# First attention stage: logits, transposes and values in turned order every second step, values one step later, dilated logits of two heads alternating

## The chip, the cores and the metric

One core of a Trainium2 chip. The metric is the device time of one execution in microseconds (us). Three executions of the kernel before were timed.

## What is computed

A model of two blocks, each of two layers, on 512 tokens of width 1024. Each layer of the first block begins with a mixer of three kinds of attention on the same normed input; the change lies in the stage that computes these, and nowhere else. The second block (stick-breaking, latent and recurrent mixers) is not touched.

```python
BLOCK = 128
def hybrid_mixer(u, pos, w_in, idx_k_norm, sinks, w_a, w_b, w_c, w_o):
    (aq, ak, av, iq, ik, iw, bq, bk, bv, cq, ck, cv, gates) = split_columns(u @ w_in)
    ...
    o_a = dsa_attention(qa, ka, av, iqr, ikr, iw * IDX_HEADS ** -0.5)   # 6 heads, keys picked by top-k
    o_b = dilated_attention(...)             # 3 groups of 4 heads: window 128 step 1, 512 step 4, 2048 step 16
    o_c = sink_window_attention(...)         # 8 heads, window 128, a sink in the denominator
    g = jax.nn.sigmoid(gates.reshape(Bsz, L, N_BRANCHES, D_MODEL))
    merged = (g[:, :, 0] * (o_a.reshape(Bsz, L, -1) @ w_a) + g[:, :, 1] * (o_b.reshape(Bsz, L, -1) @ w_b)
              + g[:, :, 2] * (o_c.reshape(Bsz, L, -1) @ w_c))
    return merged @ w_o
```

In each of the three, a block of 128 queries takes logits against its keys, a masked softmax over them, and the product of the weights with the values. The dilated one joins its three groups with weights from their log-sums; since all three are then exponentials over one common denominator, the kernel treats the keys of the three groups as one row.

## The kernel before, in words

The kernel is written engine by engine: each engine has its own queue of instructions, which it works through in order, and they meet at semaphores. The layer loop is unrolled, so the stage stands twice in the program and in the trace, with the same lines.

**Units.** The work of the stage is a list of 36 units (`units`). A unit is two heads and 128 queries: 8 dilated ones ("B", 768 logits per query: 512 of group 1, and 128 each of groups 2 and 3), 16 sliding-window ones ("C", 128 or 256 logits) and 12 top-k ones ("A", 128 to 512 logits). They are dealt in the pattern B C C A, B C C A A, so the dilated units are 0, 4, 9, 13, 18, 22, 27 and 31. The first units of each kind are short (128), the later ones longer: C is 256 wide from unit 10 on, A is 256 wide at 12, 16, 17, 384 wide at 21, 25, 26 and 512 wide at 30, 34, 35.

**Steps.** `steps()` yields for each step the unit that each stage of a software pipeline works on: s0 (this step's unit, logits), s1 (one unit back, exponentials), s2 (three back, transposes), s3 (four back, values), s4 (five back, the output's copy). All queues run over the same steps:

- TensorE: `logits(s0)`, `turn(s2)`, `values(s3)`. Logits contract over the 64 dimensions of a head, so the two heads lie on the two halves of the partitions (`half(e)`); a dilated unit makes two 512-wide products (part 0, L986) and then, head by head, two 128-wide ones for groups 2 and 3 (part 1, L991). `turn` transposes the softmax weights in blocks of 128 x 128 (L1010). `values` multiplies them with the values; the two heads write the two halves of the output's partitions (L1031).
- VectorE: for s0 a masked, scaled copy of the logits out of PSUM with a row minimum (L1119), then the minimum that ScalarE waits for (`row_min`, L1127 or L1131 to L1133; a top-k unit has only the count); for s4 the low part of the output, `o_lo` (L1143), after ScalarE's high part (`o_kept`); for s2 the copy of a dilated unit's transposes to `pt` (L1148); for s1 the reciprocal of the denominator (L1155) and, for a dilated unit, the scaling of one of its heads (L1160).
- ScalarE: for s1 the exponentials of both heads (L1066, in a window unit after the sink's at L1064), once `row_min` is there; for s4 the high part of the output, `o_hi` (L1072); for s2 the copies of the transposes of units that aren't dilated (L1079).
- GpSimd: the scaling of the other heads (L1090), after the reciprocal.
- SP: once the logits of unit 31 are done, the fetch of the next block's first weights.

**Buffers.** The eight PSUM banks are dealt round by `Banks.plan` in the order in which TensorE fills them; `bank_to_fill` waits until the bank's last content was read, `bank_filled` until it is full. The logits after the mask (`sc`) have four buffers, `pt` has two: the copy for unit k waits for the values of unit k-2.

These are the lines of VectorE's step before, in their order (bodies cut):

```python
for s0, s1, s2, s3, s4 in steps():
    if s0 is not None:   # L1119 masked copy and row minimum, then row_min
    if s4 is not None:
        dve.wait_ge(S["o_kept"], k + 1)
        nc.vector.tensor_tensor(o_lo[:, tile, cols], ...)
    if s2 is not None and pt_by_dve(s2):   # L1148 copies
    if s1 is not None:   # L1155 reciprocal, L1160 scaling
```

Of the kernel before, what the change touches and what calls it, by code (L numbers as in the profile page):

```python
# [10 lines left out]
ALU = mybir.AluOpType  # L11
# [4 lines left out]
P = 128  # L16
L = 512
D = 1024
DC = D // P
TB = L // P  # L20
# [106 lines left out]
def build(nc, d, debug=False, stop=None):  # L127
    ctx = ExitStack()
    with ctx:
# [469 lines left out]
        for layer in range(DEPTH):  # L599
# [301 lines left out]
            def steps():  # L901

                for k in range(len(units) + 5):
                    yield [k - lag if 0 <= k - lag < len(units) else None for lag in (0, 1, 3, 4, 5)]
# [13 lines left out]
            def turned(k):  # L918


                n = 2 * unit_width(units[k]) // P
                return [range(at, min(at + 4, n)) for at in range(0, n, 4)]

            jobs = Banks()
            for s0, s1, s2, s3, s4 in steps():
                if s0 is not None:
                    for part in range(2 if units[s0][0] == "B" else 1):
                        for e in range(2):
                            jobs.plan(("logits", s0, part, e))
                if s2 is not None:  # L930
                    for part in range(len(turned(s2))):
                        jobs.plan(("pt", s2, part))
                if s3 is not None:
                    jobs.plan(("o", s3))
# [23 lines left out]
            with nc.Block() as block:  # L958
# [10 lines left out]
                def _(pe, jobs=jobs):  # L969

                    def logits(k):
                        br, j, b = units[k]
                        w = unit_width(units[k])
                        for part in range(2 if br == "B" else 1):
                            for e in range(2):
# [9 lines left out]
                                elif part == 0:  # L985
# [49 lines left out]
                    for s0, s1, s2, s3, s4 in steps():  # L1035
                        if s0 is not None:
                            logits(s0)
                        if s2 is not None:
                            turn(s2)
                        if s3 is not None:  # L1040
                            values(s3)
# [52 lines left out]
                def _(dve, jobs=jobs):  # L1094
# [3 lines left out]
                    for s0, s1, s2, s3, s4 in steps():  # L1098
                        if s0 is not None:
                            k = s0  # L1100
                            br, j, b = units[k]
                            x, w = exps(k)
                            if k >= 4:

                                turn_done(dve, jobs, k - 4)
                            mn = per_unit(MIN_AT, k)
                            part0, part1 = (small[:, PART_AT + 4 * (k % 2) + 2 * i:PART_AT + 4 * (k % 2) + 2 * i + 2] for i in range(2))
                            if br == "B":
                                mask = [cst[:, C1_DIL + b * L:C1_DIL + (b + 1) * L], cst[:, C1_DIL16:C1_DIL16 + 256]]
                            elif br == "C":  # L1110
                                mask = [cst[:, C1_WIN + 256 - w:C1_WIN + 256]]
                            else:
                                mask = [causal if b == 0 else score[:, b - 1, 0:w]]
                            for part, m in enumerate(mask):
                                n = m.shape[1]
                                for e in range(2):
                                    bank = bank_filled(dve, jobs, ("logits", k, part, e))
                                    out = (mn if br == "A" else part1 if part else part0)[:, e:e + 1]
                                    i = nc.vector.tensor_tensor_reduce(out=x[:, e, part * L:part * L + n], in0=ps[:, bank, 0:n], in1=m,  # L1119
                                                                       scale=-(HD ** -0.5), scalar=-NEG, op0=ALU.add, op1=ALU.min,  # L1120
                                                                       accum_out=out)
                                    i.then_inc(read[bank], 1)
                            for part in range(len(mask)):
                                for e in range(2):
                                    dve.wait_ge(*read_of(jobs, ("logits", k, part, e)))
                            if br == "B":
# [2131 lines left out]
```

## Time and profile before

| what | us |
|---|---|
| median of 3 executions | 3410.07 |
| lowest and highest | 3406.38, 3415.58 |
| the profiled execution's own time | 3413.77 |
| its span, first to last instruction | 3411.7 |
| TensorE busy in the span | 3296.1 (97%) |
| VectorE, ScalarE, GpSimd busy | 1709.9, 1338.0, 974.0 |
| attention stage, first layer | from 228.5 to 338.4 |
| attention stage, second layer | from 1123.9 to 1235.6 |

The profile is of one execution. Busy time of TensorE is modelled: products are pipelined, and the end of one is drawn after the start of the next, so in the timeline the time from start to start is what counts. One fp32 product of logits or values leaves two records. The granted clock is the share of TensorE's full clock that the chip let it have. "Idle before" is the engine's idle time just ahead of an instruction, with what ended it; "issue" means that the profile shows nothing that was waited for.

### The profile page before, as it was taken

How to read it: one execution, taken by the hardware profiler on the slowest of the kernel's cores; microseconds unless marked ns; L12 is line 12 of the kernel's file. 1: busy time of each engine (PE TensorE's matmuls, PEld its weight loads, DVE VectorE, ACT ScalarE, POOL GpSimd, SP SyncE). 2: the span in 40 equal slices, each digit the busy share in tenths (PEclk: the TensorE clock that was granted, in tenths of full speed). 3: DMA queues.
4: the chain of work that ended last, by engine and by line, in shares of the span. 5: the costliest groups of instructions: out<-in, count | busy, mean ns of one | idle time of the engine just before them, and what ended most of it. 6: DMA issues, size and time to landing. Idle time of an engine off the chain costs nothing. (4 is left out here: it accounts for less than half of the span.)

```text
span 3411.7 us, 54710 instructions
## 1 busy us (share of the span) xinstructions
PE 3296.1 (97%) x22568; PEld 2713.9 (80%) x22568; DVE 1709.9 (50%) x2688; ACT 1338.0 (39%) x2039; POOL 974.0 (29%) x613
## 2 busy tenths in 40 slices
PE   8989999999999899999999999899999999899998
PEld 7776887888778678878887869888887768888887
DVE  5887334313259753451413675554444566454454
ACT  5647333323255553332324362343324453343322
POOL 2336002444443430034443341241101342141100
PEclk9999999999999899999999999899999999999999
DMA  4200332223221023222233100212222200112222
GB/s 158 75 25 28 105 105 88 99 88 108 88 99 62 1 80 105 104 87 99 87 125 102 62 1 4 100 50 94 91 99 95 95 1 4 76 47 103 90 95 74
DMA packets 63905, 264.36 MB, mean 77 GB/s; under 512 B 17472, under 2 KB 32192, under 8 KB 35008
## 3 DMA queue, kind: packets, MB, share of 16 engines
q1 hardware_dynamic: 63680, 261.12, 22.0%
q8 instruction: 170, 2.79, 0.4%
q14 instruction: 55, 0.45, 0.0%
HBM read 259.01 MB, written 2.10 MB: 77 GB/s over the span
## 5 line engine op out<-in xcount | busy, mean ns | idle before, releaser
L1487 POOL TENSOR_TENSOR w_lo_f<-raw_f,w_hi_f 128x2048 fp32r<-128x2048 f32 x60 | 275.7, 4596 | 379.7 <-ACT w_hi_f L389 379.7
L401 PE MATMUL ps<-u_hi,w_hi_d 128*128 128x512 f32 (+1 forms) x768 | 291.3, 379 | 7.0 <-POOL u_lo L2950 5.6
L402 PE MATMUL ps<-u_lo,w_hi_d 128*128 128x512 f32 (+1 forms) x768 | 287.3, 374 | 0.0
L403 PE MATMUL ps<-u_hi,w_lo_d 128*128 128x512 f32 (+1 forms) x768 | 287.2, 374 | 0.0
L389 ACT ACTIVATE w_hi_f<-raw_f 128x2048 fp32r<-128x2048 f32 x64 | 121.9, 1908 | 253.6 <-PE ps L403 243.8
L401 PE MATMUL ps<-hid_hi,w_hi_f 128*128 128x512 f32 x512 | 199.2, 389 | 0.0
L402 PE MATMUL ps<-hid_lo,w_hi_f 128*128 128x512 f32 x512 | 199.2, 389 | 0.0
L403 PE MATMUL ps<-hid_hi,w_lo_f 128*128 128x512 f32 x512 | 199.2, 389 | 0.0
L1514 DVE TENSOR_TENSOR hid<-hid 128x512 f32<-128x512 f32 x64 | 119.1, 1860 | 137.3 <-ACT hid L1463 135.5
L655 POOL TENSOR_TENSOR w_lo_a<-raw_a,w_hi_a 128x2048 fp32r<-128x2048 f32 x28 | 129.0, 4609 | 200.1 <-ACT w_hi_a L651 200.1
L401 PEld LDWEIGHTS ps<-u_hi,w_hi_d 128*128 128x128 f32 x768 | 146.5, 191 | 35.3 <-POOL u_lo L2950 7.4
L401 PE MATMUL ps<-u_hi,w_hi_f 128*128 128x512 f32 x448 | 174.3, 389 | 0.0
L403 PE MATMUL ps<-u_hi,w_lo_f 128*128 128x512 f32 x448 | 174.3, 389 | 0.0
L402 PE MATMUL ps<-u_lo,w_hi_f 128*128 128x512 f32 x448 | 174.3, 389 | 0.0
L1090 POOL TENSOR_SCALAR sc<-sc,small 128x256 f32<-128x256 f32 (+4 forms) x120 | 133.2, 1124 | 128.3 <-DVE small L1155 128.2
L402 PEld LDWEIGHTS ps<-u_lo,w_hi_d 128*128 128x128 f32 x768 | 147.0, 191 | 25.5 <-issue 0.5
L2962 POOL TENSOR_TENSOR hid_lo<-ge,hid_hi 128x512 f32 (+1 forms) x44 | 57.1, 1299 | 385.4 <-ACT hid_hi L2906 385.4
L403 PEld LDWEIGHTS ps<-u_hi,w_lo_d 128*128 128x128 f32 x768 | 146.9, 191 | 25.0
L395 DVE TENSOR_TENSOR w_lo_d<-raw_d,w_hi_d 128x2048 fp32r<-128x2048 f32 x44 | 106.3, 2416 | 103.9 <-ACT w_hi_d L389 103.3
L401 PE MATMUL ps<-u_hi,w_split_c 128*128 128x512 f32 x384 | 149.6, 390 | 2.1 <-SPq L228 1.0
L402 PE MATMUL ps<-u_lo,w_split_c 128*128 128x512 f32 x384 | 149.4, 389 | 0.0
L403 PE MATMUL ps<-u_hi,w_split_c 128*128 128x512 f32 x384 | 149.4, 389 | 0.0
(466 smaller groups left out, 8583.1 us busy)
## 6 DMA issues: line engine op xcount, KB each, us to landing
raw_d<-in_w SPq DMA_DIRECT2D x70, 1024.0 KB, 4.8
raw_f<-in_w SPq DMA_DIRECT2D x64, 1024.0 KB, 4.8
raw_c<-in_w SPq DMA_DIRECT2D x40, 1088.0 KB, 5.0
raw_a<-in_w SPq DMA_DIRECT2D x22, 1024.0 KB, 4.9
raw_p<-in_w SPq DMA_DIRECT2D x22, 1024.0 KB, 4.8
raw_a<-in_w SPq DMA_DIRECT2D x18, 512.0 KB, 4.8
wo_raw<-in_w SPq DMA_DIRECT2D x4, 1024.0 KB, 5.9
h<-in_x SPq DMA_DIRECT2D x8, 256.0 KB, 4.5
```

Source lines behind the costliest of these rows:

```text
L389: nc.scalar.activation(hi[:, k % 2, 0:width], raw[:, k % raw.shape[1], 0:width], ACT.Copy).then_inc(S["w_hi"], 1)
L395: nc.vector.tensor_tensor(lo[:, k % 2, 0:width], raw[:, k % raw.shape[1], 0:width], hi[:, k % 2, 0:width].bitcast(F32), ALU.subtract).then ...
L401: nc.tensor.matmul(out, w_hi, x_hi, start=start, stop=False)
L402: nc.tensor.matmul(out, w_hi, x_lo, start=False, stop=False)
L403: return nc.tensor.matmul(out, w_lo, x_hi, start=False, stop=stop)
L655: eng.tensor_tensor(WA_lo[:, i % 4, :], WA_raw[:, i % 4, :], WA_hi[:, i % 3, :].bitcast(F32), ALU.subtract)\
L1090: nc.gpsimd.tensor_scalar(x[:, e, 0:w], x[:, e, 0:w], per_unit(INV_AT, k)[:, e:e + 1], None, ALU.mult)\
L1487: nc.gpsimd.tensor_tensor(WF[2][:, k % 2, :], WF[0][:, k % 2, :], WF[1][:, k % 2, :].bitcast(F32), ALU.subtract).then_inc(S["w_lo"], 1)
L1514: nc.vector.tensor_tensor(x, x, x, ALU.mult).then_inc(S["relu_kept"], 1)
L2962: nc.gpsimd.tensor_tensor(at(hid2_lo, k), ge, at(hid2_hi, k).bitcast(F32), ALU.subtract)\
```

## The change

Three edits in this stage, and nothing outside it. TensorE's order is logits, transposes, values in even steps and values, transposes, logits in odd ones (`products()`, which the plan of the banks follows too). The lags of values and of the output's copy go from 4 and 5 to 5 and 6, so there is one step more. The four small products of a dilated unit alternate between its heads. VectorE's step is put in another order: `o_lo` comes first, then in odd steps the copy of a dilated unit's transposes, then the reduction of the logits, then in even steps that copy, and last, as before, the reciprocal. The bodies of the reduction and of the copy become functions (`reduce`, `turned_out`), unchanged. The queues of ScalarE, GpSimd and SP are not edited; they take the new lags from `steps()`.

```diff
-                for k in range(len(units) + 5):
-                    yield [k - lag if 0 <= k - lag < len(units) else None for lag in (0, 1, 3, 4, 5)]
+                for k in range(len(units) + 6):
+                    yield [k - lag if 0 <= k - lag < len(units) else None for lag in (0, 1, 3, 5, 6)]
...
-            for s0, s1, s2, s3, s4 in steps():
-                if s0 is not None:
-                    for part in range(2 if units[s0][0] == "B" else 1):
+
+            def products():
+
+                for n, (s0, s1, s2, s3, s4) in enumerate(steps()):
+                    kinds = (("logits", s0), ("turn", s2), ("values", s3))
+                    yield from (x for x in (kinds if n % 2 == 0 else kinds[::-1]) if x[1] is not None)
+
+            for what, k in products():
+                if what == "logits":
+                    for part in range(2 if units[k][0] == "B" else 1):
                         for e in range(2):
-                            jobs.plan(("logits", s0, part, e))
...
+                            if part == 1:
+                                banks = [bank_to_fill(pe, jobs, ("logits", k, part, e)) for e in range(2)]
+                                rows = slice(b, L, TB)
+                                for g in (1, 2):
+                                    for e, bank in enumerate(banks):
+                                        m = nc.tensor.matmul(ps[:, bank, (g - 1) * P:g * P], qk[half(e), T_BQ + 2 * g + j, rows],
+                                                             qk[half(e), T_BK + 2 * g + j, rows], start=(g == 1), stop=(g == 2),
+                                                             skip_group_check=True)
+                                        if g == 2:
+                                            m.then_inc(full[bank], 1)
+                                continue
...
-                                else:
-                                    for g in (1, 2):
-                                        rows = slice(b, L, TB)
-                                        m = nc.tensor.matmul(ps[:, bank, (g - 1) * P:g * P], qk[r, T_BQ + 2 * g + j, rows],
-                                                             qk[r, T_BK + 2 * g + j, rows], start=(g == 1), stop=(g == 2),
-                                                             skip_group_check=True)
-                                    m.then_inc(full[bank], 1)
...
-                    for s0, s1, s2, s3, s4 in steps():
-                        if s0 is not None:
-                            logits(s0)
-                        if s2 is not None:
-                            turn(s2)
-                        if s3 is not None:
-                            values(s3)
+                    for what, k in products():
+                        if what == "logits":
+                            logits(k)
+                        if what == "turn":
+                            turn(k)
+                        if what == "values":
+                            values(k)
...
-                    for s0, s1, s2, s3, s4 in steps():
-                        if s0 is not None:
-                            k = s0
...
+                    def turned_out(s2):
+
+                        if s2 is not None and pt_by_dve(s2):
+                            for part in range(len(turned(s2))):
+                                bank, dst, src = pt_copy(dve, jobs, s2, part)
+                                nc.vector.tensor_copy(dst, src).then_inc(read[bank], 1)
+
+                    for n, (s0, s1, s2, s3, s4) in enumerate(steps()):
                         if s4 is not None:
                             k = s4
                             bank = bank_filled(dve, jobs, ("o", k))
...
                             dve.wait_ge(S["o_kept"], k + 1)
                             nc.vector.tensor_tensor(o_lo[:, tile, cols], ps[:, bank, 0:P], o_hi[:, tile, cols].bitcast(F32),
                                                     ALU.subtract).then_inc(read[bank], 1)
-                        if s2 is not None and pt_by_dve(s2):
-                            for part in range(len(turned(s2))):
-                                bank, dst, src = pt_copy(dve, jobs, s2, part)
-                                nc.vector.tensor_copy(dst, src).then_inc(read[bank], 1)
+                        if n % 2 == 1:
+                            turned_out(s2)
+                        if s0 is not None:
+                            reduce(s0)
+                        if n % 2 == 0:
+                            turned_out(s2)
                         if s1 is not None:
                             k = s1
                             den = per_unit(DEN_AT, k)
```

## Rows read from the trace of the kernel before

**Rows 1.** Busy time by stretch: us; per engine busy (instructions); clock, DMA, GB/s.

```profile
core 0: us, PE busy (x) PEld busy (x) DVE busy (x) ACT busy (x) POOL busy (x), PEclk, DMA share, GB/s
228.50:254.20 25.70, 19.84 (x151) 15.03 (x153) 16.69 (x80) 13.79 (x50) 12.27 (x14) 0.80 0.00 1
254.20:329.60 75.40, 74.55 (x604) 51.30 (x601) 60.02 (x247) 52.50 (x167) 52.50 (x44) 0.95 0.08 31
329.60:338.40 8.80, 7.41 (x94) 5.98 (x92) 6.02 (x18) 6.13 (x16) 1.82 (x2) 1.00 0.01 3
244.00:252.00 8.00, 6.09 (x58) 4.13 (x58) 6.43 (x32) 5.72 (x26) 4.97 (x6) 1.00 0.00 1
256.00:264.00 8.00, 7.68 (x32) 4.32 (x33) 5.65 (x29) 5.98 (x22) 5.63 (x5) 0.59 0.01 3
1123.90:1153.20 29.30, 23.38 (x151) 17.12 (x153) 16.92 (x80) 13.66 (x50) 12.30 (x14) 0.71 0.00 1
1153.20:1226.80 73.60, 71.72 (x604) 49.57 (x601) 59.69 (x246) 52.21 (x167) 52.48 (x44) 1.00 0.08 32
```

**Rows 2.** Timeline of TensorE, first layer: start, length in us, line, records.

```profile
269.42 0.70 PE L982 MATMUL ps<-qk 64*128 64x256 f32 x4
270.06 0.66 PE L1010 MATMUL ps<-cst,sc 128*128 128x128 f32 x4
271.23 0.70 PE L982 MATMUL ps<-qk 64*128 64x256 f32 x4
...
305.14 1.30 PE L991 MATMUL ps<-qk 64*128 64x128 f32 x8
306.38 0.66 PE L1010 MATMUL ps<-cst,sc 128*128 128x128 f32 x4
```

**Rows 3.** Waits of the values' weight loads, 228.5 to 338.4 us: total us, times, longest.

```profile
PEld ps L1031 <- issue: 6.3, 34, 0.4
```

**Rows 4.** Timeline of VectorE, first layer: start and length in us.

```profile
280.41 0.69 DVE L1119 CUSTOM_DVE_ANT_0 sc<-ps,cst 128x512 f32<-128x512 f32 x1 [1.55 <-PE ps L986]
...
284.95 0.29 DVE L1143 TENSOR_TENSOR o_lo<-ps,o_hi 128x128 fp32r<-128x128 f32 x1 [0.17 <-ACT o_hi L1072]
285.16 0.15 DVE L1155 RECIPROCAL small<-small 128x2 f32<-128x2 f32 x1
...
289.21 1.88 DVE L1148 COPY pt<-ps 128x512 f32<-128x512 f32 x3
...
297.11 0.42 DVE L1119 CUSTOM_DVE_ANT_0 sc<-ps,cst 128x256 f32<-128x256 f32 x1
...
298.97 0.56 DVE L1119 CUSTOM_DVE_ANT_0 sc<-ps,score 128x384 f32<-128x384 f32 x1
...
325.78 0.69 DVE L1119 CUSTOM_DVE_ANT_0 sc<-ps,score 128x512 f32<-128x512 f32 x1 [0.47 <-PE ps L979]
```

**Rows 5.** Timeline of ScalarE, first layer.

```profile
282.74 0.94 ACT L1066 ACTIVATE sc<-sc,small 128x768 f32<-128x768 f32 x1
...
284.59 0.25 ACT L1072 ACTIVATE o_hi<-ps 128x128 fp32r<-128x128 f32 x1
...
298.38 0.20 ACT L1064 ACTIVATE small<-small 128x2 f32<-128x2 f32 x1
...
299.47 0.25 ACT L1072 ACTIVATE o_hi<-ps 128x128 fp32r<-128x128 f32 x1
...
300.09 0.61 ACT L1066 ACTIVATE sc<-sc,small 128x384 f32<-128x384 f32 x1 [0.37 <-DVEq L1136]
...
301.31 0.25 ACT L1072 ACTIVATE o_hi<-ps 128x128 fp32r<-128x128 f32 x1
...
327.17 0.72 ACT L1066 ACTIVATE sc<-sc,small 128x512 f32<-128x512 f32 x1 [0.95 <-DVEq L1136]
...
328.60 0.25 ACT L1072 ACTIVATE o_hi<-ps 128x128 fp32r<-128x128 f32 x1
```

**Rows 6.** Timeline of GpSimd, first layer: both heads of a 256-wide unit.

```profile
291.45 1.83 POOL L1090 TENSOR_SCALAR sc<-sc,small 128x256 f32<-128x256 f32 x2 [1.62 <-DVE small L1155]
```

More of the change, by code:

```diff
@@ L924, in build @@
             jobs = Banks()
[L925 to L934 removed]
+            def products():
[5 more added lines that the diff above has]
+                    for part in range(2 if units[k][0] == "B" else 1):
+                        for e in range(2):
+                            jobs.plan(("logits", k, part, e))
+                if what == "turn":
+                    for part in range(len(turned(k))):
+                        jobs.plan(("pt", k, part))
+                if what == "values":
+                    jobs.plan(("o", k))
             def o_place(unit):
@@ L1097, in _ @@
                                                                 prm[:, P1_SINK:P1_SINK + C_HEADS], -1.0, None, ALU.mult)))
-                    for s0, s1, s2, s3, s4 in steps():
-                        if s0 is not None:
-                            k = s0
[L1101 to L1126, printed above, removed]
-                                nc.vector.tensor_tensor(mn, part0, part1, ALU.min).then_inc(S["row_min"], 1)
-                            elif br == "C":
-                                sink = slice(2 * j, 2 * j + 2)
-                                dve.wait_ge(*own.up(nc.vector.tensor_tensor(mn, part0, prm[:, P1_NSINK:P1_NSINK + C_HEADS][:, sink],
-                                                                            ALU.min)))
-                                nc.vector.tensor_tensor(per_unit(SINK_AT, k), mn, prm[:, P1_SINK:P1_SINK + C_HEADS][:, sink],
-                                                        ALU.add).then_inc(S["row_min"], 1)
-                            else:
-                                dve.sem_inc(S["row_min"], 1)
@@ new lines, in reduce @@
+                    def reduce(k):
+                        br, j, b = units[k]
+                        x, w = exps(k)
+                        if k >= 4:
+                            turn_done(dve, jobs, k - 4)
+                        mn = per_unit(MIN_AT, k)
+                        part0, part1 = (small[:, PART_AT + 4 * (k % 2) + 2 * i:PART_AT + 4 * (k % 2) + 2 * i + 2] for i in range(2))
+                        if br == "B":
+                            mask = [cst[:, C1_DIL + b * L:C1_DIL + (b + 1) * L], cst[:, C1_DIL16:C1_DIL16 + 256]]
+                        elif br == "C":
+                            mask = [cst[:, C1_WIN + 256 - w:C1_WIN + 256]]
+                        else:
+                            mask = [causal if b == 0 else score[:, b - 1, 0:w]]
+                        for part, m in enumerate(mask):
+                            n = m.shape[1]
+                            for e in range(2):
+                                bank = bank_filled(dve, jobs, ("logits", k, part, e))
+                                out = (mn if br == "A" else part1 if part else part0)[:, e:e + 1]
+                                i = nc.vector.tensor_tensor_reduce(out=x[:, e, part * L:part * L + n], in0=ps[:, bank, 0:n], in1=m,
+                                                                   scale=-(HD ** -0.5), scalar=-NEG, op0=ALU.add, op1=ALU.min,
+                                                                   accum_out=out)
+                                i.then_inc(read[bank], 1)
+                        for part in range(len(mask)):
+                            for e in range(2):
+                                dve.wait_ge(*read_of(jobs, ("logits", k, part, e)))
+                        if br == "B":
+                            nc.vector.tensor_tensor(mn, part0, part1, ALU.min).then_inc(S["row_min"], 1)
+                        elif br == "C":
+                            sink = slice(2 * j, 2 * j + 2)
+                            dve.wait_ge(*own.up(nc.vector.tensor_tensor(mn, part0, prm[:, P1_NSINK:P1_NSINK + C_HEADS][:, sink],
+                                                                        ALU.min)))
+                            nc.vector.tensor_tensor(per_unit(SINK_AT, k), mn, prm[:, P1_SINK:P1_SINK + C_HEADS][:, sink],
+                                                    ALU.add).then_inc(S["row_min"], 1)
+                        else:
+                            dve.sem_inc(S["row_min"], 1)
```

7 lines of the change are left out of this document (3 added, 4 removed).

## Prediction

> **What bounds the kernel now.** I read the busy time of each engine by stretches first, for this stage alone. The attention stage runs once per layer of the first block, twice in all. Its steady stretch, from the start of VectorE's first logits reduction of unit 9 to that of unit 35, lasts 75.4 us in the first layer and 73.6 us in the second; before it lie 25.7 us of start-up, behind it 8.8 us of tail [rows 1]. The reader is to see that TensorE is busy for 74.55 of 75.40 us there, while VectorE has 60.02, ScalarE 52.50 and GpSimd 52.50: TensorE sets the pace and each other engine has room, if its work may overlap. Then the timeline of TensorE: a step of a 256-wide unit (logits, transposes, values) goes from 269.42 to 271.23, which is 1.81 us [rows 2]. Then the waits of the weight loads: before values, whose kind of product differs from what ran before, they sit for nothing the profile shows, 0.19 us at a time (6.3/34) [rows 3]. I take that as the price of going from one kind of product to another.
>
> **What the change takes out of TensorE.** Turning every second step round puts values beside values and logits beside logits: two changes of kind per step in place of three, some 36 x 0.19 = 6.8 us per layer. The two heads' dilated logits alternate: four 128-column products take 1.24 us (305.14 to 306.38), two of 256 columns on the two halves 0.64 us (269.42 to 270.06) [rows 2]. The same columns can't cost less than the latter, so each of 8 dilated units saves between 0 and 0.60 us, at most 4.8 us per layer. The Trainium skill (TensorE: Matmul & The Clock Gate, What overlaps and what doesn't) says that a weight load overlaps running products only if its row group differs. By that rule the sum for TensorE would stand at the 4.8 us end, and these rows agree. I cost both savings at nothing in the total, because the next part takes TensorE off the path.
>
> **What the change adds: a wait at the head of VectorE's step.** Values move from lag 4 to lag 5, the write of o_lo from 5 to 6, and on VectorE o_lo moves ahead of the reduction of this step's logits. ScalarE's queue is not reordered: in step n it does the exponentials of unit n-1, then o_hi of unit n-6, then its copies of transposes. VectorE's step n now begins with o_lo of unit n-6, which waits for that o_hi. It stands behind the exponentials of n-1, and these need the row minimum of n-1 from VectorE's step before. So from step 6 on each reduction starts only when the exponentials of the unit before are done: reduce(n-1), exp(n-1), o_hi, o_lo, reduce(n), one after another on two engines. Before, reduce(n) ran beside exp(n-1), and only o_lo, behind it, waited. Queued behind the wait are now the dilated copy (odd steps), the reduction, the reciprocal and the scaling; ScalarE waits for them, GpSimd for the reciprocal, TensorE for GpSimd and for banks.
>
> One link of this chain, from reduction to reduction, for each kind of unit:
> - Sliding-window unit, 256 wide: reduction at 297.11, ScalarE starts at 298.38 (1.27); o_hi starts at 299.47 and takes 0.25 (1.34) [rows 4, 5]. From the end of an o_hi (284.59 + 0.25) to its o_lo at 284.95 is 0.11, and what follows an o_lo starts 0.21 later (285.16) [rows 4, 5]. Together 2.93.
> - Dilated: 280.41 to 282.74 (2.33), to the end of o_hi at 284.84 (2.10), plus 0.32: 4.75.
> - Top-k unit, 384 wide: 298.97 to 300.09 (1.12), to 301.56 (1.47), plus 0.32: 2.91. 512 wide: 325.78 to 327.17 (1.39), to 328.85 (1.68), plus 0.32: 3.39. For 256 I take as much less again, 2.43 [rows 4, 5].
>
> Units 9 to 34 lead from reduce(9) to reduce(35): 6 dilated, 12 window, 3 + 3 + 2 top-k units: 28.5 + 35.2 + 7.3 + 8.7 + 6.8 = 86.5 us. The copies of dilated units (three in 1.88 us [rows 4]) come on top. In odd steps they now stand between o_lo and the reduction, for units 18 and 22: 2 x 1.88 = 3.8. In even steps they run while ScalarE works and stick out: 1.88 plus some 0.4 for the reciprocal and its neighbours, against ScalarE's part of the link, leaves about 0.85 with a 256-wide and 0.4 with a 512-wide unit, two of each: 2.5. Sum 92.8 us, which is 17.4 over the first layer's 75.4 and 19.2 over the second's 73.6.
>
> Start-up: logits of step 3 now stand behind the transposes of unit 0, and the copies of units 0 and 4 before reduce(3) and reduce(7). This can cost nothing or both copies, 3.8 us; I take 1.8 in the first layer. In the second, whose start-up is already 3.6 us longer (29.3 against 25.7 us [rows 1]), I take 0, with the same two ends. Tail: one step more, with little in it. It lies between nothing and a values block with its copies, 2 us; I take 1 each. SP's fetch of the next weights waits for the logits of unit 31 and moves with them, four links ahead of its first reader: nothing. If that cover went, the next block would wait for it. GpSimd keeps its 52.5 us of work inside 92.8: nothing.
>
> Total: 17.4 + 1.8 + 1 + 19.2 + 0 + 1 = 40.4 us. Against the profiled execution's own 3413.77 us (span 3411.7 and 2.1 around it) this is 3454.2. That execution lies 3.7 us above the median of the three runs, so against the median the forecast is 3410.07 + 40.4 = **3450 us**, 1.2% slower. A measurement of this kernel can tell about 0.3%, 10.2 us, from no change.
>
> **Rivals.** *TensorE stays the bound, faster.* If ScalarE reached o_hi before VectorE needs it, the step would be TensorE's, and both savings would count: 6.8 and up to 4.8 us per layer, 23 us in all, 3387 us. The place is the gap at each change of kind [rows 3]; the point is where a link becomes shorter than TensorE's step. Against it: 2.93 us against 1.81. The Trainium skill (TensorEngine Tiling (Array Packing), Key Properties) says that a change of tiling mode drains TensorE. By that rule alone the change would win, at the 3387 us just given; the 0.19 us gaps agree with it. Chance 0.04.
>
> *GpSimd's scaling becomes the wait, the chain through o_lo does not bind.* Transposes of an even unit now come a step earlier after the odd unit's logits. From those logits it takes 1.27 and some 0.2 us on VectorE, then two heads in 1.83 us on GpSimd [rows 6], 3.3 us; TensorE has a logits, a transposes and two values blocks to do, 0.64 + 0.58 + 1.0 = 2.2 us [rows 2]. 1.1 us are missing in the 7 of 13 pairs of steps without long work to cover it, 8 us per layer; about 7 come back as fewer changes of kind (13 x 2 x 0.19 = 4.9) and as alternation. The time would be about 3412 us, the same by measure. For it: the loop is there. Against it: the other one is longer, 5.86 us for two window steps against 3.3 + 0.58 + 0.64 = 4.5. Chance 0.05.
>
> *The clock falls too.* Between 244 and 252 us TensorE was busy for 6.09 of 8 us at the full clock; from 256 to 264 it was granted 0.59 on average, between its levels of 1.2 and 2.4 GHz [rows 1]. With the chain it would be busy for 71.7 of 92.8 us, a share like that before the fall. At the lower level TensorE's work doubles, so it becomes the bound again if over 0.29 of its 71.7 us falls there (92.8/71.7 - 1). With half of it there, the stretch is 107.6 us, 14.8 more per layer: 3480 us. For it is the start-up of either layer, granted 0.80 in the first; against it, the clock came back, since the whole stretch has 0.95 and the second layer's 1.00. Chance 0.08.
>
> **How the numbers follow.** The chain has 0.83. Its own range: 3434 with no odd or even copies in the chain, no start-up cost and no tail; 3456 with both copies in both start-ups. The range given, 3432 to 3472, adds part of the clock's case and leaves out the two quicker rivals. Faster by over 0.3% has 0.04, within 0.3% 0.05, slower 0.91.
>
> **What would show it.** In the changed profile o_lo should have a long idle time before it, ended by ScalarE's o_hi, in nearly every step from 6 on, some 1 us with a window unit; ScalarE's exponentials should wait for VectorE's row minimum. From reduce(9) to reduce(35) should be about 93 us, with one window step near 2.9 us, and TensorE should show idle time before logits and transposes. The four dilated products should take between 0.64 and 1.24 us. The prediction is wrong if o_lo waits little, if the stretch stays near 75 us, or if TensorE is busy throughout at a low clock.

## The result, and the profile after

The changed kernel takes 3501.82 us (median of 4 runs, 3493.79 to 3505.21) beside 3410.26 us of the kernel before on the same chip: ratio 1.0267, 95% interval 1.0252 to 1.0282. It is slower by 91.6 us; the forecast was slower by 40.4 us. The direction was right, the size was not, and 3502 lies outside the range of 3432 to 3472.

The busy time by stretch of the changed kernel, with the columns of [rows 1]; in order, start-up, steady stretch and tail of the first layer, then start-up and steady stretch of the second:

```profile
228.20:260.80 32.60, 22.68 (x154) 16.67 (x156) 16.94 (x80) 13.83 (x50) 12.32 (x14) 0.69 0.00 1
...
260.80:374.70 113.90, 79.27 (x602) 59.31 (x598) 59.65 (x247) 52.81 (x167) 53.29 (x45) 0.84 0.06 21
...
374.70:384.70 10.00, 7.03 (x93) 6.07 (x93) 6.08 (x17) 5.54 (x15) 1.48 (x2) 1.00 0.01 2
...
1170.60:1203.00 32.40, 23.47 (x154) 17.23 (x156) 17.02 (x80) 13.87 (x50) 12.32 (x14) 0.63 0.00 1
...
1203.00:1317.50 114.50, 78.88 (x602) 59.33 (x598) 59.61 (x246) 52.94 (x167) 53.21 (x45) 0.85 0.05 21
```

Against [rows 1] the steady stretch grew by 38.5 us (113.90 - 75.40) and 40.9 us (114.50 - 73.60), the start-up by 6.9 us (32.60 - 25.70) and 3.1 us (32.40 - 29.30), and the tail of the first layer by 1.2 us. These account for nearly all of the 91.6 us: the loss is in this stage. VectorE, ScalarE and GpSimd have the work they had, to within 1 us; TensorE is busy for 79.27 of 113.90 us in place of 74.55 of 75.40, at a granted clock of 0.84. So no engine is full: the stage waits.

The waits of the changed kernel from 228 to 390 us (total us, times, longest):

```profile
DVE o_lo L1162 <- ACT o_hi L1083: 51.6, 30, 4.3
PE ps L1021 <- DVE o_lo L1162: 30.1, 11, 4.0
ACT pt L1090 <- PE ps L1042: 27.5, 11, 4.5
PEld ps L1021 <- POOL sc L1101: 24.3, 11, 4.4
ACT sc L1077 <- DVEq L1146: 22.5, 10, 4.3
ACT sc L1077 <- DVE small L1137: 16.1, 6, 3.8
ACT small L1075 <- DVE small L1143: 11.1, 10, 1.6
PE ps L1042 <- DVE o_lo L1162: 7.5, 4, 2.4
```

The first row is the forecast chain: VectorE's o_lo at the head of its step waits for ScalarE's o_hi in 30 of 36 steps, and the exponentials (L1075, L1077) wait for VectorE's minima. Three more kinds of wait have no price in the forecast: TensorE's transposes (L1021) and its values (L1042) wait for o_lo, and ScalarE's copies (L1090) wait for TensorE's values. Two steps of the timeline, 280.66 to 286.77 and 286.77 to 289.79, show how they hang together (start, length in us, engine and line; in brackets the idle time before it and what ended it):

```profile
280.66 0.29 DVE L1162 TENSOR_TENSOR o_lo<-ps,o_hi 128x128 fp32r<-128x128 f32 x1 [2.17 <-ACT o_hi L1083]
281.10 1.08 PE L1021 MATMUL ps<-cst,sc 128*128 128x128 f32 x4 [4.01 <-DVE o_lo L1162]
282.11 2.50 PE L1042 MATMUL ps<-pt,bv 128*64 128x128 f32 x24
...
284.72 0.60 ACT L1090 ACTIVATE pt<-ps 128x512 f32<-128x512 f32 x1 [4.16 <-PE ps L1042]
285.22 0.19 ACT L1075 ACTIVATE small<-small 128x2 f32<-128x2 f32 x1
...
286.29 0.38 ACT L1083 ACTIVATE o_hi<-ps 128x128 fp32r<-128x128 f32 x1
...
286.77 0.39 DVE L1162 TENSOR_TENSOR o_lo<-ps,o_hi 128x128 fp32r<-128x128 f32 x1 [3.95 <-ACT o_hi L1083]
...
289.43 0.25 ACT L1083 ACTIVATE o_hi<-ps 128x128 fp32r<-128x128 f32 x1
289.79 0.29 DVE L1162 TENSOR_TENSOR o_lo<-ps,o_hi 128x128 fp32r<-128x128 f32 x1 [1.21 <-ACT o_hi L1083]
```

From 286.77 to 289.79 is a window step that is the chain and nothing else: 3.02 us, where 2.93 were forecast. From 280.66 to 286.77 is one of 6.11 us. Step 14 begins it: o_lo of unit 8 ends and frees its PSUM bank. The transposes of unit 11 were dealt that very bank, so TensorE stood idle for 4.01 us until then. The transposes run at the lower clock of 1.2 GHz (granted 0.50 from 281.10 to 282.11): 1.08 us, where four take 0.66 at the full clock in [rows 2]. The values of unit 9 run mostly at it (granted 0.59 from 282.11 to 284.60): 2.50 us, where the kernel before takes 1.53 us for such values at the full clock:

```profile
267.96 1.53 PE L1031 MATMUL ps<-pt,bv 128*64 128x128 f32 x24
```

ScalarE's copy of unit 11 goes into the operand buffer that the values of unit 9 still read, one of two, so it starts after them, at 284.72. The exponentials of unit 14 stand behind this copy, o_hi of unit 9 behind the exponentials, and the next o_lo behind that. So a second loop goes o_lo, bank, transposes and values, copy, exponentials, o_hi, o_lo; where it closes here, the step is twice as long. The wait of this copy for the values is not needed for the loop: experiment 7 takes it away and gains little.

The order in which the kernel deals its banks fixes how often such a meeting comes. In the changed kernel 13 products per layer are dealt a bank whose last content is an output with its o_lo in the same step; 11 of them are transposes, as many as the waits of L1021 for o_lo. With the old order and the same lags there is none.

### The profile page after: what moved, and what is told of

Its sections match the earlier page's. It is cut to its first block and busy times, and to the rows that moved or that the text cites. A ratio compares the mean times of both kernels' runs of the same rounds, so it can differ in the third digit from the quotient of the medians.

```text
span 3503.4 us, 54724 instructions
## 1 busy us (share of the span) xinstructions
PE 3310.3 (94%) x22568; PEld 2735.3 (78%) x22568; DVE 1709.0 (49%) x2688; ACT 1338.0 (38%) x2039; POOL 974.9 (28%) x613
```

## The experiments

None of these kernels leaves out anything that the reference computes. They undo or do one part each. "Before" is the run of the kernel before on the same chip.

**1. The split first, alone.** On the kernel before, only VectorE's o_lo moves ahead of the reduction; lags, order and banks stay.

```diff
 for s0, s1, s2, s3, s4 in steps():
+    if s4 is not None:
+        dve.wait_ge(S["o_kept"], k + 1)
+        nc.vector.tensor_tensor(o_lo[...], ...)
     if s0 is not None:
```

> The kernel before with one edit: VectorE writes o_lo ahead of the reduction of the step's logits. Order of TensorE, lags, banks as before. Theory: the chain is there without the turned order; links of 86.5 us from unit 9 to 34 and about 5 us of dilated copies that stick out, against 75.4 and 73.6 us now: 3435 to 3455 us. Rival (the turned order is what costs): 3405 to 3415 us, as before.

Measured: 3452.75 us, before 3410.78, ratio 1.0125 [1.0108, 1.0142]: 42 us slower. Busy time of its steady stretch in the first layer, columns as in [rows 1]:

```profile
258.30:349.70 91.40, 76.52 (x607) 51.74 (x608) 58.66 (x247) 52.67 (x167) 53.05 (x45) 0.94 0.07 26
```

The longest wait of its stage, VectorE's o_lo for ScalarE (total us, times, longest, as in all fences of waits):

```profile
DVE o_lo L1105 <- ACT o_hi L1072: 36.5, 27, 2.4
```

What follows: the chain exists, and the sum of its links was right: 91.4 us (92.6 in the second layer), where this run's own expectation of 86.5 and about 5 us makes 91.5. But it is worth 42 us, not 92.

**2. Values one step later, alone.** On the kernel before, lags 5 and 6 in place of 4 and 5. Then the same with two short operand buffers more, for units of up to 256 columns, so that nearly every copy waits for values of four units before.

```diff
-    yield [... for lag in (0, 1, 3, 4, 5)]
+    yield [... for lag in (0, 1, 3, 5, 6)]
```
```diff
+pt_short = [place("pt_2", 38584, 512), place("pt_3", 34488, 512)]
-b, m, _ = jobs.at["o", k - 2]
+b, m, _ = jobs.at["o", PT_BEFORE[k]]
```

> The kernel before with nothing changed but the values (and with them the split of their output) one step later, lags 5 and 6 in place of 4 and 5; order of the kinds, VectorE's places and the alternation as before. Theory (ScalarE's copy into the values' operand buffer, of which there are two, now waits for values of its own step, and the next exponentials stand behind it): slower, about where the run with the order of before and the new lags was (3443), that is 3435 to 3450, with ScalarE's copies ended by TensorE's values in 20 us or more of the stage of layer 1, where the kernel before shows little of this. Rival (a later step only gives slack; what cost there was VectorE's split behind the reduction with two banks): 3405 to 3415.

> The kernel before with the values one step later, as in the run with that alone, and two short buffers more for the values' operand, so that a copy waits for values of four units before in nearly all cases. Theory (the loss by the lag alone is the wait of the copies on the two buffers): back to 3405 to 3416, ScalarE's copies no longer ended by values. Rival (the loss by the lag alone is something else, as the output's bank held a step longer): within 5 us of the run with the lag alone.

Measured: the later step alone 3424.49 us, before 3412.2, ratio 1.0038 [1.0024, 1.0051]; with more buffers 3411.48 us, ratio 0.9994 [0.9985, 1.0004]. The waits of ScalarE's copies with the later step alone:

```profile
ACT pt L1079 <- PE ps L1031: 27.5, 18, 3.3
```

With more buffers no such row is left; the copies wait only for their own transposes, as in the kernel before:

```profile
ACT pt L1090 <- PE ps L1021: 19.3, 15, 5.1
```

What follows: the later step costs 12 us, less than the 23 to 38 that the theory's 3435 to 3450 make, and all of it by the two buffers, as the theory had it. The forecast had counted the later values as moving o_lo's lag and had not looked at the buffers.

**3. The turned order.** First alone: on the kernel before, with the alternation, VectorE's copies at their new places and two banks for the values alone, but the old lags and the split behind the reduction. Then the other way round: the changed kernel with the old order in every step, all else as changed.

```diff
-kinds if n % 2 == 0 else kinds[::-1]
+kinds
```

> The kernel before with the turned order of logits, transposes and values in every second step, VectorE's copies at their places of after, the alternation and banks of their own for the values, but with the old lags 4 and 5 and the split behind the reduction: the turned order without the later step. Theory (in a step pair the values of two units then stand next to each other, and the second waits for transposes made right ahead of them to be copied out by ScalarE, over 1 us at each pair, with the split behind a reduction that waits for logits behind the values): slower, 3440 to 3480. Rival (the order alone saves its 0.19 us at each change of kind and costs nothing): 3400 to 3411.

> The changed kernel with logits, transposes, values in this order in every step; split first on VectorE, values one step later, alternation and VectorE's copies as changed, banks shared as in the kernel before. Theory (38 us of the loss come from the turned order: it deals the banks so that transposes meet a bank that is freed only behind the split at the head of the same step): the sum of the two single costs, 3410 + 42 + 12 = 3464, within 12. Rival (split first and later values lengthen each other through the shared banks whatever the order): 3485 or more.

Measured: the order alone 3475.58 us, before 3412.2, ratio 1.018 [1.0163, 1.0197]; the changed kernel with the old order 3458.9 us, before 3411.95, ratio 1.0141 [1.0125, 1.0158]. Waits with the order alone:

```profile
PE ps L1043 <- DVE o_lo L1167: 21.3, 20, 1.9
...
PEld ps L1043 <- ACT pt L1091: 16.2, 10, 2.1
```

Waits of the changed kernel with the old order:

```profile
DVE o_lo L1162 <- ACT o_hi L1083: 40.5, 31, 3.7
...
ACT pt L1090 <- PE ps L1042: 17.5, 11, 3.8
...
PE ps L1021 <- DVE o_lo L1162: 2.8, 4, 1.8
```

Busy time of its steady stretch:

```profile
257.30:352.40 95.10, 79.30 (x628) 52.60 (x626) 58.93 (x248) 52.47 (x167) 53.24 (x46) 0.93 0.07 25
```

What follows: this is the run that divides the loss. In the old order split and later step together cost 47.0 us (3458.9 - 3411.95); turning the order adds 44.6 (91.6 - 47.0), give or take some 8 us by the two intervals. The transposes' waits for o_lo fall from 30.1 to 2.8 us when the order is turned back. Turning the order without the later step is worse still, 63 us slower, but that run has a second cost in it: its o_lo stands behind the reduction, and values wait for it for 21.3 us. The first kernel of experiment 6 differs from it by the later step alone and is 46.7 us slower than before (3456.99 - 3410.26). So the missing step accounts for some 17 of the 63 us; there values stand right behind the transposes' copies and wait for ScalarE (16.2 us).

**4. Cutting the loops in the changed kernel.** ScalarE's o_hi ahead of its exponentials cuts the chain; banks 6 and 7 for the values alone, the other six for the rest, cut the bank loop.

```diff
 for s0, s1, s2, s3, s4 in steps():
+    o_hi(s4)
     exps(s1)
-    o_hi(s4)
```
```diff
-jobs = Banks()
+jobs = Banks(count=6)
-jobs.plan(("o", k))
+jobs.fills[6 + k % 2] += 1
+jobs.at["o", k] = (6 + k % 2, jobs.fills[6 + k % 2], 0)
```

> The changed kernel with one edit: ScalarE writes o_hi before the exponentials of the step, not behind them. Theory (the serial chain reduce, exp, o_hi, o_lo, reduce, which the banks make worse): the chain is cut, o_lo's waits on o_hi fall from 52 us per layer to under 10, and the time falls by at least 80 us, to between 3385 and 3420 us. Rival (the turned order itself costs the time, by GpSimd's scaling that must now fit between logits and the next transposes but one): the time stays over 3470 us, and transposes wait for GpSimd as long as now.

> The changed kernel with one edit: values have two PSUM banks of their own (one for even, one for odd units), everything else goes round in the other six. Theory (the chain costs some 40 us, and what lies above it is TensorE waiting for banks that the late o_lo holds, which holds up transposes, ScalarE's copies and so the exponentials): TensorE's waits on o_lo, 40 us per layer, nearly vanish, and the time falls to 3440 to 3465 us. Rival A (the banks only show the chain's lateness): 3490 to 3510 us. Rival B (without the banks there is no chain either): under 3420 us.

> The changed kernel with both cuts: ScalarE writes o_hi before the exponentials, and values have two PSUM banks of their own. Theory (two costs, the chain through o_hi and the banks that o_lo holds, and nothing else): from reduce(9) to reduce(35) 70 to 76 us, TensorE's waits on o_lo under 3 us per layer, 3395 to 3415 us in all. Rival (the turned order itself is slower, GpSimd's scaling between logits and transposes): the stretch stays over 79 us, 3420 us or more, with transposes waiting for GpSimd over 8 us per layer.

Measured: o_hi first 3438.57 us, ratio 1.0079 [1.0062, 1.0096]; own banks 3465.95 us, ratio 1.0158 [1.0141, 1.0175] (before 3410.78 for both); both 3427.93 us, before 3410.26, ratio 1.0054 [1.0038, 1.0071]. The waits in the first layer's stage with o_hi first:

```profile
DVE o_lo L1162 <- ACT o_hi L1074: 13.4, 12, 2.4
...
PE ps L1021 <- DVE o_lo L1162: 10.9, 9, 1.6
```

The same waits with own banks:

```profile
DVE o_lo L1163 <- ACT o_hi L1084: 39.4, 31, 2.3
...
PE ps L1043 <- DVE o_lo L1163: 17.6, 13, 3.2
```

Busy time of the steady stretch with own banks:

```profile
259.40:354.70 95.30, 73.81 (x602) 52.78 (x600) 59.01 (x247) 51.70 (x166) 52.98 (x45) 0.93 0.07 25
```

The longest waits with both cuts:

```profile
PEld ps L1022 <- POOL sc L1102: 12.5, 17, 2.8
PE ps L1022 <- POOL sc L1102: 9.5, 10, 2.0
DVE o_lo L1163 <- ACT o_hi L1075: 5.9, 6, 1.7
...
PE ps L1043 <- DVE o_lo L1163: 4.3, 6, 1.2
```

What follows: with own banks the stretch falls from 113.9 to 95.3 us, that of the changed kernel in the old order with shared banks (95.1): the chain is left, the second loop is gone (36 us in all). The values still wait for o_lo for 17.6 us, against the expectation, so a wait for o_lo does not cost its length by itself. Cutting the chain is worth more, 63 us; read from the queues, the bank loop passes through the same exponentials and is loosened with it. The expectation was 80 us at least, and o_lo still waits for o_hi for 13.4 us where under 10 were expected. Both cuts together give 74 us, not 99: the two loops share links. They miss the expected 3395 to 3415 us as well. The rival's sign, transposes waiting for GpSimd for over 8 us, is there, and experiment 8 tries it.

**5. Controls.** On the kernel before, only the banks for values; and only the alternation of the dilated logits.

> The kernel before with one edit: values have two PSUM banks of their own, the rest goes round in six. A control: what the banks alone do. Theory (in the order of before no bank is held up long): within 6 us of before, 3404 to 3416 us. Rival (six banks for logits and transposes are too few): 3420 us or more. Rival (banks cost the kernel before too): under 3400 us.

> The kernel before with one edit: the four small products of a dilated unit alternate between the two heads. If they run beside each other on the halves of the array, they take 0.64 to 0.87 us in place of 1.24, which is worth 16 x 0.37 to 16 x 0.60, 6 to 10 us: 3400 to 3404 us. Rival (the strided reads or the weight loads bound them): 1.1 to 1.24 us, under 2 us in all, 3408 to 3412 us.

Measured: the banks 3410.8 us, ratio 1.0002 [0.9992, 1.0011]; the alternation 3410.27 us, ratio 0.9996 [0.9987, 1.0006]. TensorE's timeline with the alternation, the eight records of four products and what follows them:

```profile
264.15 1.09 PE L980 MATMUL ps<-qk 64*128 64x128 f32 x8
...
265.18 0.66 PE L1014 MATMUL ps<-cst,sc 128*128 128x128 f32 x4
```

What follows: neither hides a gain or a loss of its own; the 6 to 10 us expected of the alternation did not come. Four alternating products take 1.03 us (265.18 - 264.15) in place of 1.24 [rows 2], 0.21 of the 0.60 that were possible at most.

**6. The split behind the reduction again, with own banks**, in the turned and then in the old order. (With shared banks this was not tried: by the plan of the banks the small logits of unit 22 are dealt the bank that the o_lo of the same step frees. That o_lo would stand behind the reduction of these very logits, and each engine would wait for the other.)

```diff
-    o_lo(s4)
     reduce(s0)
+    o_lo(s4)
```

> The changed kernel with o_lo back behind the reduction, as in the kernel before, and two PSUM banks of their own for values, without which TensorE and VectorE would wait for each other there. The turned order, the lags and the alternation stay. Theory: as the run with o_hi first and own banks, 3395 to 3415 us, since the chain is cut at its other end. Rival (the place of o_lo does not matter, only ScalarE's order does): 3460 us or more. Rival (GpSimd's loop): 3415 to 3430 us.

> As the run with o_lo back and own banks, but TensorE's order is logits, transposes, values in every step; lags and alternation stay. It tells the turned order from the rest: if turning saves changes of kind, 0.19 us each, this run is slower than that one by up to 13 us. Theory: slower by 3 to 13 us. Rival (what turning saves is lost again to GpSimd's tighter loop): the same within 3 us, or faster.

Measured: 3456.99 us, ratio 1.0134 [1.0117, 1.0151]; in the old order 3443.38 us, ratio 1.0099 [1.008, 1.0118] (before 3410.26). Both expectations of the theory fell: o_lo's place does not give the time back, and the old order is the faster one by 13.6 us, not the slower. The longest wait of TensorE in the first kernel, values for o_lo:

```profile
PE ps L1043 <- DVE o_lo L1167: 23.5, 23, 2.3
```

In the old order ScalarE's copies wait longest, for values:

```profile
ACT pt L1091 <- PE ps L1043: 26.2, 15, 3.5
```

What follows: values in the turned order wait for o_lo, and turning costs 13.6 us in this place of o_lo too. A reading of the queues, which no run tests by itself, is another loop in place of the old one: values at the head of an odd step need one bank of two, the o_lo that frees it stands behind a reduction, and the logits of that reduction stand behind earlier values. In the old order the wait for the two operand buffers is left. But that run is 33 us slower than before and the later step alone 12 us (experiment 2); the other 21 us, which come with the banks, the alternation and the new places of VectorE's copies, are not divided further.

**7. More operand buffers in the changed kernel**, alone and with both cuts of experiment 4.

> The changed kernel with nothing but two short buffers more for the values' operand, so that ScalarE's copies wait for values of four units before in nearly all cases and not of the step they stand in. Theory (in the changed kernel these copies wait mostly for transposes that are late by the bank and chain loops, 27.5 us a stage, and the buffers add a little on top): 3485 to 3500. Rival (the wait for values of the same step is a link of the long loop bank, values, copy, exponentials): 3455 to 3480.

> The changed kernel with ScalarE's o_hi ahead of its exponentials, banks of their own for the values (3428 so far) and two short buffers more for the values' operand (for units of up to 256 columns), so that a copy waits for values of four units before in nearly all cases. Theory (copies held by the values are a small part of what is left, 5 us a stage in the trace of that run, GpSimd's scaling loop and the start and end are the rest): 3418 to 3426, copies on ScalarE no longer ended by values. Rival (these copies were the head of the chain that was left): 3400 to 3415, about the kernel before or below.

Measured: alone 3494.38 us, before 3411.95, ratio 1.0247 [1.023, 1.0264], some 7 us better than the changed kernel, though the two intervals overlap; with both cuts 3420.05 us, before 3412.2, ratio 1.0026 [1.0016, 1.0036]. Two waits of the first kernel, and the step of unit 15 in it:

```profile
PE ps L1032 <- DVE o_lo L1173: 29.4, 11, 4.0
ACT pt L1101 <- PE ps L1032: 22.3, 18, 2.4
```
```profile
283.61 0.39 DVE L1173 TENSOR_TENSOR o_lo<-ps,o_hi 128x128 fp32r<-128x128 f32 x1 [2.67 <-ACT o_hi L1094]
...
285.88 0.42 DVE L1140 CUSTOM_DVE_ANT_0 sc<-ps,cst 128x256 f32<-128x256 f32 x1 [1.88 <-PE ps L1011]
...
288.60 0.29 DVE L1173 TENSOR_TENSOR o_lo<-ps,o_hi 128x128 fp32r<-128x128 f32 x1 [1.21 <-ACT o_hi L1094]
```

Two steady stretches can be compared at the full clock. The first is that of the later step with more buffers on the kernel before (experiment 2, old order):

```profile
252.40:327.40 75.00, 72.47 (x618) 50.48 (x619) 59.60 (x247) 53.04 (x169) 53.55 (x46) 1.00 0.08 31
```

The second is that of the changed kernel with all three loops cut (turned order):

```profile
255.40:331.00 75.60, 65.31 (x602) 48.31 (x600) 59.20 (x246) 51.13 (x166) 52.41 (x45) 1.00 0.08 31
```

What follows: the buffers are a small part of the loss in the changed kernel, as expected, and the copy's wait for values is not a link that the second loop needs. Without it the transposes wait for o_lo as long as they did (29.4 us for 30.1), the copies wait for the transposes, and the loop finds a second way. In the turned order the logits of an odd step stand behind the values and transposes, so the reduction of unit 15 now waits 1.88 us for them, and its step takes 4.99 us (288.60 - 283.61) where it took 3.02. The step before it is shorter, but the two together, from the o_lo at 278.78, take 9.82 us where they took 9.13 (289.79 - 280.66).

With all loops cut TensorE is busy for 7.2 us less per stage (72.47 - 65.31). Not all of this is saved work: 16 products' records fewer lie in the stretch (618 and 602), since the turned order moves some across its ends, by estimate 1.9 us (16 x 72.47/618). Some 5.3 us are left. And yet the stretch is as long as the 75.4 us of the first layer before: TensorE waits in place of working.

**8. What is left.** The reciprocal of the unit before ahead of the reduction in odd steps; VectorE scaling one head of every even unit in place of GpSimd; both. All with the three loops cut.

```diff
+    if n % 2 == 1:
+        scales(s1)
     reduce(s0)
-    scales(s1)
+    if n % 2 == 0:
+        scales(s1)
```
```diff
-BY_DVE = [... if unit[0] == "B" or k >= len(units) - 2]
+BY_DVE = [... if unit[0] == "B" or k % 2 == 0 or k >= len(units) - 2]
```

> The changed kernel with all three loops cut (ScalarE's o_hi first, banks of their own for the values, more operand buffers: 3420) and, in odd steps, VectorE's reciprocal and scaling of the unit before ahead of the reduction of the next, where VectorE waits for logits anyway. Theory (what is left is GpSimd's scaling, let go too late: 15.7 us of waits of transposes for it in the stretch): 3390 to 3412, the transposes' waits for GpSimd below 8 us. Rival (the reduction then waits for the exponentials of the unit before, a serial chain again): 3422 to 3440.

> The changed kernel with all three loops cut (3420) and VectorE scaling one of the two heads of every even unit, whose transposes come early in the odd steps; GpSimd keeps the other. Theory (the transposes of these units wait for GpSimd, 15.7 us in the stretch, because it scales two heads of 0.92 us one after the other): those waits under 6 us, time 3390 to 3410. Rival (the wait is for the reciprocal that comes late, not for the scaling; VectorE only gets more to do): 3414 to 3430.

> The same with VectorE's reciprocal and scaling of the unit before ahead of the reduction in odd steps. Theory (both the late reciprocal and GpSimd's two heads hold the transposes): 3385 to 3405, below the run with the sharing alone. Rival (the reduction waits for the exponentials, as in the run with the reciprocal first alone, 3422): 3412 to 3430.

Measured: 3421.6 us, before 3411.95, ratio 1.003 [1.0019, 1.0042]; 3419.8 us, before 3408.07, ratio 1.0028 [1.0017, 1.0039]; both 3432.33 us, ratio 1.0066 [1.0049, 1.0083]. TensorE's waits for GpSimd from 255 to 331 us with the loops cut alone, 7.0 us of products and 8.7 us of weight loads:

```profile
PE ps L1033 <- POOL sc L1113: 7.0, 9, 1.5
...
PEld ps L1033 <- POOL sc L1113: 8.7, 14, 1.8
```

The same with the scaling shared:

```profile
PE ps L1033 <- POOL sc L1113: 4.8, 6, 1.5
...
PEld ps L1033 <- POOL sc L1113: 4.3, 5, 1.6
```

What follows: the theory fell. The 15.7 us in the expectations add the waits of products to those of weight loads, and in the timeline these are largely the same waits seen twice (a product at 311.32 after 1.51 us, its weight load at 311.32 after 1.75); the products alone wait 7.0 us. Sharing the scaling takes that to 4.8 us and the time stays; the earlier reciprocal alone changes nothing either, and with the sharing it makes things worse. So neither of the two is what holds the last version at 75.6 us, as far as they take effect: 4.8 us of the products' waits for GpSimd are still there. What holds it is open, and no version here is faster than the kernel before.

## Why the prediction was right and wrong

- **The chain through o_hi.** Right, in kind and in size: a plain window link takes 3.02 us for 2.93, and o_lo first alone makes a stretch of 91.4 and 92.6 us for 92.8, 42 us in all for 40.4. That the totals come so close is partly luck, since the kernel of experiment 1 has no dilated copies ahead of its reductions and the forecast has 3.8 us for them.
- **The turned order, costed at nothing.** This is the step that failed. The forecast took its saving of TensorE's time as hidden behind the chain and asked nothing more of it. Turning the order costs 44.6 us on top of the rest (experiment 3), because the shared banks are dealt in the order of the products: in the new order transposes meet the bank of values whose o_lo stands at the head of the same VectorE step, 11 times per layer. With banks of their own for the values the stretch is 95.3 us, the same as in the old order. "TensorE [waits] for GpSimd and for banks" stood in the text, as a consequence only; that this wait leads back into the chain, by copy and exponentials or by the logits behind the transposes, was not followed. The stretch was 21 us per layer longer than the chain.
- **The values one step later.** Counted for o_lo's lag alone. With two operand buffers a copy then waits for values of its own step: 12 us alone, and some 7 of the changed kernel's loss, which the intervals do not set clear of nothing.
- **Start-up and tail.** Forecast 1.8 and 0 us, measured 6.9 and 3.1; the first layer's is above even its upper end of 3.8. Tail forecast 1, measured 1.2.
- **TensorE's savings.** The forecast of 36 x 0.19 us by fewer changes of kind was about right as work: of the estimated 5.3 us, 6 x 0.21 = 1.3 are the alternation of the stretch's six dilated units, and 4.0 are left for 26 steps, 0.15 each. The Trainium skill (TensorEngine Tiling (Array Packing), Key Properties) has a change of mode drain the engine, and this work that went agrees; the win of time that the rule alone would give did not come in any run. For the alternation the forecast had between 0 and 0.60 us per unit, and 0.21 was measured. The Trainium skill (TensorE: Matmul & The Clock Gate, What overlaps and what doesn't) lets a weight load overlap running products only if its row group differs; the forecast took this, and its rows, to speak for the 0.60 us end, and that was wrong.
- **The rivals.** TensorE as the bound, and GpSimd alone: excluded by the idle time of TensorE and by experiment 4; the wait for GpSimd is TensorE's longest only with both cuts made. The clock: it did fall, to 0.84. In the 6.11 us step it makes 0.4 us of the transposes (1.08 - 0.66) and 1.0 of the values (2.50 - 1.53), 1.4 of the 3.1 us by which this step is longer than the plain one. But TensorE is busy for only 79.27 of 113.90 us; had it been the bound, as that rival had it, TensorE would have no idle time.

How much of the 44.6 us is the lower clock and how much the banks was not measured apart: the cuts that remove the bank loop also bring the clock back, to 0.93 with own banks and to 1.00 with all loops cut. The rows set a limit. Between the changed kernel and own banks, with the same 602 records, TensorE's busy time falls by 5.5 us (79.27 - 73.81) and the stretch by 18.6, so at least 13 us of that per layer are waiting and not slower work. That the clock fell because of the waits, and not the other way round, is argued from this and not shown: no run moves the clock alone.

## What to carry to other kernels

When a change reorders one engine's queue, write down for each shared resource (PSUM banks, operand buffers, score buffers) who frees it and in which step under the new order, and follow each such wait round until it ends or comes back; a wait that comes back is a loop, and its length is the step. Two loops that share links do not add up: here the single costs are 42 and 12 us and the turned order 45, cutting either loop gives back 36 or 63, and both 74. A later step for one kind of work is only slack if its buffers are a step deeper too.

## What the runs showed of the hardware that was not expected

- Alternating the two row halves of four 128-column products gives 1.03 in place of 1.24 us, where two 256-column products on the two halves take 0.64 [rows 2].
- TensorE kept a granted clock of 1.00 over a stretch in which it was busy for 65.31 of 75.60 us and its products waited for up to 1.5 us at a time, and was granted 0.84 over one in which it was busy for 79.27 of 113.90 us and they waited for up to 4.0 us. After one of these, from 281.10 to 282.11, four transposes went at the lower clock of 1.2 GHz.
